# Gate tables of a product-key mixture built eight tokens at a time in 16-bit numbers by VectorE, one Trainium2 core

## What is computed

```python
s1, i1 = lax.top_k(s[:, :, 0], PEER_TOPK)
s2, i2 = lax.top_k(s[:, :, 1], PEER_TOPK)
...
gate = jax.nn.softmax(top_s, axis=-1)
...
act = gelu(einsum('pkd,pd->pk', expert_u[ib], tb)) * gb
return einsum('pk,pkd->pd', act, expert_v[ib])
```

## Time and profile before

| | |
|---|---|
| median of three runs | 4902.4 us |
| profiled execution | 4900.0 us, of which the span 4898.2 |
| PE busy | 3926.4 us, 80%, 20597 instructions |
| DVE busy | 2314.9 us, 47%, 5082 |
| ACT busy | 1610.8 us, 33%, 3031 |
| gate tables, call 1 | 1226.8 to 1426.9 us |
| gate tables, call 2 | 2824.1 to 2924.4 us |
| mean granted TensorE clock | 0.886 |

### The profile page before, as it was taken

One profiled execution on the slowest core, in us unless ns is written; L12 is line 12 of the kernel. 1 busy time (PEld: TensorE's weight loads), 2 busy tenths in 40 slices (PEclk: granted clock), 3 DMA queues, 4 the chain that ended last, 5 costly groups with the idle time before them and its releaser, 6 DMA issues. The chain is left out here.

```text
span 4898.2 us, 61331 instructions
## 1 busy us (share of the span) xinstructions
PE 3926.4 (80%) x20597; PEld 2742.5 (56%) x20597; DVE 2314.9 (47%) x5082; ACT 1610.8 (33%) x3031; POOL 170.6 (3%) x148
## 2 busy tenths in 40 slices
PE   5988997977749999999869667999727677776776
PEld 2448996433647878888646557999615522222222
DVE  0435663177866666666525876888253200000001
ACT  1223342011864444444314175666112111111111
POOL 0003441000000000000000000000000000000000
PEclk7978998988989999999989788999856897888888
DMA  7200001042355545544320139998221189999996
GB/s 273 69 0 1 1 1 69 36 172 76 114 168 187 179 179 180 180 171 171 117 97 16 63 101 346 317 317 290 94 111 57 35 360 427 427 427 428 427 428 275
DMA packets 302749, 905.03 MB, mean 185 GB/s; under 512 B 18672, under 2 KB 138736, under 8 KB 277104
## 3 DMA queue, kind: packets, MB, share of 16 engines
q1 hardware_dynamic: 302576, 902.68, 48.8%
HBM read 851.24 MB, written 51.38 MB: 184 GB/s over the span
## 5 line engine op out<-in xcount | busy, mean ns | idle before, releaser
L1655 PE MATMUL pd<-h_parts,u_parts 128*128 128x512 f32 x2048 | 485.3, 396 | 45.5 <-DVE u_parts L1741 45.5
L1668 PE MATMUL po<-act_parts,v_parts 128*128 128x512 f32 x2048 | 482.8, 393 | 9.9 <-DVE v_parts L1746 7.4
L1655 PEld LDWEIGHTS pd<-h_parts,u_parts 128*128 128x128 f32 x2048 | 385.2, 188 | 140.0 <-DVE u_parts L1741 45.7
L2764 PE MATMUL pb<-moe_ring,moe_xs 128*32 128x512 f32 x2048 | 336.4, 764 | 137.0 <-DMA moe_ring<-in_moe_gu 120.6
L1668 PEld LDWEIGHTS po<-act_parts,v_parts 128*128 128x128 f32 x2048 | 384.0, 189 | 104.2 <-DVE v_parts L1746 21.7
L2815 DVE TENSOR_TENSOR moe_hidden<-moe_silu,pg 128x512 f32<-128x512 f32 x16 | 11.0, 688 | 654.3 <-PE pg L2753 486.7
L1861 PE MATMUL pd<-h_parts,u_parts 128*128 128x256 f32 x2048 | 265.7, 284 | 43.3 <-DVE u_parts L1940 43.3
L1861 PEld LDWEIGHTS pd<-h_parts,u_parts 128*128 128x128 f32 x2048 | 262.4, 192 | 53.5 <-DVE u_parts L1940 43.8
L289 PE MATMUL ps<-hT,w_stream 128*128 128x512 f32 (+1 forms) x672 | 267.4, 561 | 27.8 <-ACTq L309 27.8
L1483 PE MATMUL ps<-first_ind,second_ind 128*128 128x128 f32 x1536 | 223.7, 298 | 77.8 <-DVE second_ind L1469 48.5
L1483 PEld LDWEIGHTS ps<-first_ind,second_ind 128*128 128x128 f32 x1536 | 196.8, 203 | 105.1 <-issue 68.6
(11 more groups left out here) (449 smaller groups left out, 6317.6 us busy)
## 6 DMA issues: line engine op xcount, KB each, us to landing
moe_ring<-in_moe_gu SPq DMA_DIRECT2D x128, 2048.0 KB, 26.7
u_stream<-in_peer_u SPq DMA_DIRECT2D x256, 512.0 KB, 6.3
v_stream<-in_peer_v SPq DMA_DIRECT2D x256, 512.0 KB, 5.0
moe_ring<-in_moe_down SPq DMA_DIRECT2D x64, 2048.0 KB, 26.2
ada_ring<-in_ada_w SPq DMA_DIRECT2D x24, 2048.0 KB, 17.2
peer_gates<-gate_stage SPq DMA_DIRECT2D x6, 8192.0 KB, 30.3
g_stream<-peer_gates SPq DMA_DIRECT2D x128, 256.0 KB, 5.0
w_stream<-in_gdn_w_in SPq DMA_DIRECT2D x8, 2048.0 KB, 8.4
```

Of the source, the lines that this page charges most:

```text
L1655: m = pe.matmul(pd[:, j, 0:T], us[:, j, w, c], h[:, w, c], start=(c + w == 0), stop=(c == DC - 1 and w == 1))
L1668: m = pe.matmul(po[:, (c + b) % 4, 0:T], vs[:, j, w, (c + b) * P:(c + b) * P + P], aparts[:, 4 * half + j, w], start=(j + w == 0), stop=(j ...
L2764: m = pe.matmul(pb[32 * q:32 * q + 32, n % 2, :], xs[:, u % 2, c], w[:, c, :], start=(c < 4), stop=(c >= 4))
```

## The change

`peer_scatter` is rewritten; `peer_layer` and everything else stay. At the head of a call VectorE makes `numbers`, a 16-bit table [128 keys, 8] of the key numbers with each repeated for 8 tokens, and `keys`, the two rows of keys in 16-bit numbers. Then one loop over all turns; a turn is 16 tokens still, now two halves of 8. For each half VectorE compares `numbers` with the second and the first keys (two 16-bit tables, key by key with the token innermost), and multiplies the second one by the weights into B, float32, token by token. ScalarE turns the first one into A, float32, token by token ("widening"), and evacuates the four banks as before. All tables have two buffers. TensorE's matmuls and SyncE's writes are as they were. The sums of the semaphores at the end follow.

Removed lines are cut to the first of each run, for they are printed above.

```diff
@@ -1430,127 +1430,115 @@
 def peer_scatter(k, selT, T, consts, gates):
     nc = k.nc
     C = lambda name: CONSTS(consts, name)
     tiles = T // P
-    SETS = 4
-    GROUP = 4 * SETS
+    SET = 8
+    GROUP = 2 * SET
     TURNS = P // GROUP
-    ind_b, joined, taken, squared = (k.sig(x) for x in ("sc_second", "sc_joined", "sc_taken", "sc_squared"))
...
+    ALL = tiles * TURNS
+    first, widened, second, gated, joined, taken = (
+        k.sig("sc_" + x) for x in ("first", "widened", "second", "gated", "joined", "taken"))
+    ready = k.sig("sc_keys")
     written = [k.sig("sc_written0"), k.sig("sc_written1")]
     with ExitStack() as ctx:
         stage = k.sb(ctx, "gate_stage", [2, P, P])
-        dist = k.sb(ctx, "first_distance", [2, 4, P])
...
+        numbers = k.sb(ctx, "key_numbers", [P, SET], BF16)
+        keys = k.sb(ctx, "keys_16", [2, T], BF16)
+        is_first = k.sb(ctx, "is_first", [2, P, SET], BF16)
+        is_second = k.sb(ctx, "is_second", [2, P, SET], BF16)
+        A = k.sb(ctx, "first_ind", [2, SET, P])
+        B = k.sb(ctx, "second_ind", [2, SET, P])
         ps = k.banks(ctx, 4)
+        def here(i, x):
+            return bass.ds(i * GROUP + SET * x, SET)
         with nc.Block() as block:
             @block.vector
             def _(dve):
-                dve.sem_inc(ind_b.h, SETS)
...
+                dve.sem_inc(gated.h, 2)
+                dve.tensor_copy(numbers[:], C("iota").rearrange("p (n a) -> p n a", a=1).broadcast_to([P, P, SET]))
+                dve.tensor_copy(keys[:], selT[:, 0:2, :]).then_inc(ready.h, 1)
+                dve.wait_ge(ready.h, ready.at(1))
+                with dve.Fori(0, ALL) as i:
+                    for x in range(2):
+                        def marks(row):
+                            return keys[:, row, here(i, x)].rearrange("p (n a) -> p n a", n=1).broadcast_to([P, P, SET])
+                        dve.wait_ge(gated.h, gated.at(1 + x) + i * 2)
+                        dve.tensor_tensor(is_second[:, x], numbers[:], marks(1), ALU.is_equal).then_inc(second.h, 1)
+                        dve.wait_ge(widened.h, widened.at(1 + x) + i * 2)
+                        dve.tensor_tensor(is_first[:, x], numbers[:], marks(0), ALU.is_equal).then_inc(first.h, 1)
+                        dve.wait_ge(second.h, second.at(1 + x) + i * 2)
+                        dve.wait_ge(joined.h, joined.at(2 * x + 2) + i * 4)
+                        gate = selT[:, 2, here(i, x)].rearrange("p (a n) -> p a n", n=1).broadcast_to([P, SET, P])
+                        dve.tensor_tensor(B[:, x], is_second[:, x].rearrange("p n a -> p a n"), gate, ALU.mult).then_inc(gated.h, 1)
             @block.tensor
             def _(pe):
-                for tile in range(tiles):
...
+                pe.sem_inc(joined.h, 4)
+                with pe.Fori(0, ALL) as i:
+                    for b in range(4):
+                        x = b // 2
+                        if b % 2 == 0:
+                            pe.wait_ge(widened.h, widened.at(3 + x) + i * 2)
+                            pe.wait_ge(gated.h, gated.at(3 + x) + i * 2)
+                        pe.wait_ge(taken.h, taken.at(1 + b) + i * 4)
+                        for a in range(4):
+                            n = 4 * (b % 2) + a
+                            m = pe.matmul(ps[:, b, a * P:a * P + P], B[:, x, n], A[:, x, n], start=True, stop=True)
+                        m.then_inc(joined.h, 1)
             @block.scalar
             def _(act):
-                act.sem_inc(taken.h, SETS)
...
+                act.sem_inc(taken.h, 4)
+                act.sem_inc(widened.h, 2)
+                def widen(i, x):
+                    act.wait_ge(first.h, first.at(1 + x) + i * 2)
+                    act.wait_ge(joined.h, joined.at(2 * x + 2) + i * 4)
+                    act.activation(A[:, x], is_first[:, x].rearrange("p n a -> p a n"), ACT.Copy).then_inc(widened.h, 1)
+                def take(i, tile, at, b):
+                    act.wait_ge(joined.h, joined.at(5 + b) + i * 4)
+                    act.activation(stage[:, tile % 2, :, bass.ds(at + 4 * b, 4)], ps[:, b, :].rearrange("p (t n) -> p n t", t=4), ACT.Copy).then_inc(taken.h, 1)
                 for tile in range(tiles):
                     t0 = tile * TURNS
-                    copy_picks(t0, tile * P)
...
+                    widen(t0, 0)
+                    widen(t0, 1)
                     if tile >= 2:
                         act.wait_ge(written[tile % 2].h, written[tile % 2].at(DMA_DONE * (tile // 2)))
-                    def turn_of(i, at, last):
...
+                    take(t0, tile, 0, 0)
+                    take(t0, tile, 0, 1)
+                    with act.Fori(0, TURNS - 1) as n:
+                        i = n + t0
+                        at = n * GROUP
+                        widen(i + 1, 0)
+                        take(i, tile, at, 2)
+                        take(i, tile, at, 3)
+                        widen(i + 1, 1)
+                        take(i + 1, tile, at + GROUP, 0)
+                        take(i + 1, tile, at + GROUP, 1)
+                    take(t0 + TURNS - 1, tile, P - GROUP, 2)
+                    take(t0 + TURNS - 1, tile, P - GROUP, 3)
             @block.sync
             def _(sp):
                 for tile in range(tiles):
-                    sp.wait_ge(taken.h, taken.at(SETS + (tile + 1) * TURNS * SETS))
+                    sp.wait_ge(taken.h, taken.at(4 + (tile + 1) * TURNS * 4))
                     sp.dma_start(gates[:, :, tile * P:tile * P + P].rearrange("i p t -> p i t"), stage[:, tile % 2]).then_inc(written[tile % 2].h, DMA_DONE)
                 for w in written:
                     sp.wait_ge(w.h, w.at(DMA_DONE * tiles // 2))
```

More of the change, by code:

```diff
@@ L1505, in indicate @@
-                def indicate(turn, b):
-                    act.wait_ge(squared.h, squared.at(3 + b // 2) + turn * 2)
-                    act.activation(A[:, 4 * b:4 * b + 4], dist[:, b // 2], ACT.Relu, bias=1.0, scale=-1.0).then_inc(ind_a[0].h, 1)
-                def take(n, tile, at, b):
-                    act.wait_ge(joined.h, joined.at(1) + n)
-                    act.activation(stage[:, tile % 2, :, bass.ds(at, 4)], ps[:, b, :].rearrange("p (t n) -> p n t", t=4), ACT.Copy).then_inc(taken.h, 1)
+                act.sem_inc(taken.h, 4)
@@ L1513, in _ @@
                 for tile in range(tiles):
                     t0 = tile * TURNS
-                    copy_picks(t0, tile * P)
-                    for b in (0, 2):
-                        square(t0, b)
-                    for b in (0, 2):
-                        indicate(t0, b)
+                    widen(t0, 0)
+                    widen(t0, 1)
                     if tile >= 2:
                         act.wait_ge(written[tile % 2].h, written[tile % 2].at(DMA_DONE * (tile // 2)))
-                    def turn_of(i, at, last):
-                        if not last:
-                            copy_picks(i + (t0 + 1), tile * P + GROUP + at)
-                        for b in (0, 2):
-                            take(i * SETS + (SETS * t0 + b), tile, at + 4 * b, b)
-                            if not last:
-                                square(i + (t0 + 1), b)
-                            take(i * SETS + (SETS * t0 + b + 1), tile, at + 4 * b + 4, b + 1)
-                            if not last:
-                                indicate(i + (t0 + 1), b)
@@ L1544, in _ @@
                     sp.wait_ge(w.h, w.at(DMA_DONE * tiles // 2))
-    n = tiles * TURNS * SETS
-    for b in range(2):
-        ind_a[b].done(n // 2)
-    squared.done(n // 2 + 2)
-    ind_b.done(n + SETS)
-    picks.done(tiles * TURNS)
-    copied.done(tiles * TURNS)
-    joined.done(n)
-    taken.done(n + SETS)
+    ready.done(1)
+    for x in (first, second):
+        x.done(2 * ALL)
+    for x in (gated, widened):
+        x.done(2 * ALL + 2)
+    for x in (joined, taken):
+        x.done(4 * ALL + 4)
     for w in written:
```

19 lines of the change are left out of this document (removed).

## The result

The changed kernel takes 4909.44 us (median of 20 runs, 4904.11 to 4916.72) against 4900.66 for the kernel before on the same chips (20 runs): a ratio of 1.002, interval 1.0013 to 1.0027. That is 8.8 us or 0.18% by the medians, against a forecast of 4908 and +8.4. The profiled execution has a span of 4906.8 us, 8.6 above the one before.

A forecast was written before the change was run, and what follows sets the result against it. VectorE was taken to bound the gate stage; turns of 6.24 us for 5.92, with setup and tail and less tile openings, gave +4.4 us in call 1 and +4.0 in call 2: 4900.0 + 8.4 = 4908 us, range 4838 to 4945.

The forecast's parts named there:

- VectorE bounds the turn, before and after: Gate stage, turn of 16 tokens: VectorE's instructions fill it, 5.92 us before the change and 6.24 after.
- The comparisons at 0.60 from start to start: VectorE's two 16-bit comparisons per 8 tokens: 692 ns each as in L1408, 1.20 us for both.
- The multiplication at 1.81 ns an element from L1414: VectorE's multiplication, reading is_second at 16-byte steps: 2.01 us for 1024 elements, 1.92 from start to start.
- L1396's 2.16: Rival, step dearer: VectorE's multiplication at 2.16 ns an element takes 2.37 us, a turn 6.96, total 4943 us; chance 0.17.
- The widening at VectorE's price: ScalarE's two widenings a turn, reading at 16-byte steps: VectorE's 1.81 ns an element, about 2.0 us each.
- ScalarE's 5.9 a turn: ScalarE's widenings and evacuations: 5.9 us a turn, hidden behind VectorE by 0.3 only.
- The openings vanish into the slack: Tile openings: the 2.7 us a tile spent on ScalarE's opening vanish, as VectorE runs on and only its sum counts.
- 2 us of cover: VectorE's wait for TensorE to release a table buffer (`joined`): free, with 2 us to spare.
- Setup: Once a call, VectorE's casts `numbers` and `keys`: 0.60 + 0.69 + 0.1 us in call 1, 0.60 + 0.42 + 0.1 in call 2.
- The sign by which ScalarE was to be caught: TensorE's waits: put down to `second_ind` in the forecast case, to `first_ind` if ScalarE's widening takes the stage over.
- the widening bound the turn: Rival on ScalarE: from 2.0 ns an element its turn passes 6.24; at 2.16 it is 6.6, total 4925 us; chance 0.06.
- The free step: Rival: VectorE's multiplication pays nothing or nearly so for 16-byte steps, 1.22 us long, a turn 4.8, total 4843 us; chance 0.22.

The follow-up runs named there:

- widen_dense: Changed kernel with ScalarE's widening reading is_first densely in memory order, A not transposed: 4906.75 us against 4903.17 for the kernel before.
- step_8_bytes: Changed kernel with its 16-bit tables as two groups of four tokens, reads stepping 8 bytes, computation whole: 4834.09 us against 4900.90 for the kernel before.
- mult_dense: Changed kernel with VectorE's multiplication reading is_second densely in memory order, B not transposed: 4896.71 us against 4903.17 for the kernel before.
- smooth_opening: Changed kernel with a tile's last two evacuations put between the next tile's two widenings on ScalarE: 4908.32 us against 4903.17 for the kernel before.
- both_dense: Changed kernel with multiplication and widening both reading densely, neither table transposed: 4837.23 us against 4903.17 for the kernel before.

## Why the prediction was right, and where it was not

- **The number.** 8.8 us by the medians for a forecast of 8.4, but 12.0 by the two calls themselves. The closeness is in part luck; the terms below are what can be judged.
- **VectorE bounds the turn, before and after.** Right. Before by its sum in the earlier trace rows; after by a window without idle time, and by `widen_dense`, where halving ScalarE's largest instruction brought 3 to 5 us.
- **The comparisons at 0.60 from start to start.** Right, 694 ns long, from L1408.
- **The multiplication at 1.81 ns an element from L1414.** Right to 0.2%, 2013 for 2.01. It was also the step on which the sign hung, and here too there was luck: the row steps 32 bytes, no row stepped 16, and none could tell whether 16 bytes would cost what 32 do or nothing, as 8 do (`step_8_bytes`). L1396's 2.16, a step on the written side, did not apply. The 1.73 that the Trainium skill lists ("Vector Engine (DVE) Microarchitecture Reference", section 5.2) would have put the sum 8 us lower; the row was the better price.
- **The widening at VectorE's price.** Right, 2060 for "about 2.0", though no row of ScalarE showed a step. ScalarE's 5.9 a turn stayed hidden, as `mult_dense` shows: uncovered, it holds the turn at 5.85.
- **The openings vanish into the slack.** This step failed, by 2.9 us in call 1. The prediction had VectorE run on through an opening with 2 us of cover. But ScalarE's two widenings in a row make TensorE 1.6 us late, which leaves 0.24 us of it even at the full clock (the second tile's opening, no wait), and at a granted clock of 0.50 the 16 instructions took 1.6 us longer, which VectorE waited for. The cover was named, and what an opening takes of it was not asked. `smooth_opening` takes exactly this away: its call 1 lasts 204.3 us, for a forecast of 204.2.
- **Setup.** 1.64 us from the first cast to the first comparison in call 1 and 1.39 in call 2, where 1.4 and 1.1 were counted: the self-wait costs 0.34, not 0.1.
- **The sign by which ScalarE was to be caught was wrong.** The prediction said that TensorE's waits would go to `second_ind`, and to `first_ind` if the widening bound the turn. They went to `first_ind` while VectorE bound it. Two engines make tables for the same product, and the row names whichever ends last, 0.27 us apart; it doesn't say which of them is full.
- **The free step** got 0.22 and was not the case at 16 bytes. Its working was good: 4843 for a measured 4837 (`both_dense`).

## What to carry to other kernels

Before a transposing read of 16-bit elements, count the bytes of a step: to 8 bytes it was free on VectorE and nearly so on ScalarE, at 16 they took 1.65 and 1.95 times as long, and splitting the group of tokens from eight into two fours moved the hop to where it costs nothing. Price a step from the nearest row of the trace that has one, even a small helper of 32 elements, and ask whether the row lies on the same side of a stair. And when two engines are nearly level, make each one's instruction cheap alone and then both together: here that gave 15, 5 and 75 us. Before trusting an overlap at a loop's edge, work out how much of the cover the edge itself takes.

## What the runs showed that was not expected

- The price of a step is a stair: 1219, 2013 and 2035 ns for 1024 elements at 8, 16 and 32 bytes on VectorE, 1161, 2060 and 2071 on ScalarE. On the written side a run of 8 bytes is free (686 ns) and one of 4 costs 1.78 ns a pair (1063). Single elements written 8 bytes apart are another case: L1396 has 2.16 ns each, and no run tried why.
- ScalarE pays the same absolute price as VectorE, 1.84 ns an element ((2060 - 180)/1024), although its dense rate is 0.85 and VectorE's 1.04.
- The Trainium skill, "SBUF — State Buffer", in its note on cachelines, has it that accesses are at full rate from two hits on a 16-byte line. By that, steps of 8 bytes in 16-bit numbers (two to a line) are free and steps of 16 are not. The runs agree on both sides of the stair for reads; L1396's writes at steps of 8 bytes do not. The same note has 8 bf16 elements as a stride that is free, and that is the step of 16 bytes that took 2013 ns: there the measurement decides. The Trainium skill's "Vector Engine (DVE) Microarchitecture Reference", section 5.2, speaks of pairs of 4-byte words instead, from streams of 32-bit numbers; by that a step of 8 bytes, each element in a pair of its own, would not be dense, and 1219 ns says that it is.
- With 16-bit products TensorE's granted clock was 0.50 in this window where its reads stepped 16 bytes, and it was busy throughout; it was 0.71 where they stepped 8 and it was busy for 37.59 of 44 us. Why was not tried. It cost nothing there: 16 instructions took 2.05 us at 0.50 and 2.04 at 1.00, where in float32 the openings of the changed kernel show 3.6 us at 0.50 and 2.0 at 1.00.
